# The differential-attention mixer of a two-block network: from projections first and attention second, to attention by pairs of heads beside the projections

## The reference, cut to what matters

```python
def mixer_ab(hx, hc, ...):      # 256 tokens, 256 context rows, D = 1024
    lam = exp(sum(lq1 * lk1)) - exp(sum(lq2 * lk2)) + lam_init
    q_x, k_x, v_x, gu_x, gv_x = split(hx @ w_in)     # 8 heads x 2 x 64; v: 8 x 128
    q_x, k_x = apply_rope(q_x), apply_rope(k_x)
    k_c, v_c = split(hc @ w_in[:, QK_W:2 * QK_W + V_W])
    k_all, v_all = concat(k_c, k_x), concat(v_c, v_x)        # 512 keys
    # per block of 128 queries and per head:
    p = softmax(q @ k.T * scale)             # two maps of 128 x 512
    a = p[:, :, 0] - lam * p[:, :, 1]
    o_x = a @ v
    a_x = o_x * rsqrt(mean(o_x * o_x) + eps) * norm_g * (1 - lam_init)   # per head
    u, v = gelu(gu_x), layer_norm(gelu(gv_x))
    g_x = u * (w_s @ v + b_s)
    return concat(a_x, g_x) @ w_out
```

## Time and profile before

| | |
|---|---|
| median of 3 runs | 2221.75 us (2221.7 to 2222.33) |
| profiled execution, its own time | 2223.49 us |
| its span | 2221.7 us |
| TensorE busy over the span | 1822.1 us (82%) |
| VectorE / ScalarE busy | 1471.4 us (66%) / 877.2 us (39%) |
| the mixer stage in it | 413.7 to 729.1 us |

### The profile page before, as it was taken

The page is one execution under the profiler, slowest core; times in us unless marked ns, Lnnn a source line. Parts: engine busy times, 40 slices in busy tenths (PEclk is TensorE's granted clock), DMA queues, the critical chain, the costliest instruction groups (busy, mean ns, idle before and its releaser), DMA issues.

```text
span 2221.7 us, 21883 instructions
## 1 busy us (share of the span) xinstructions
PE 1822.1 (82%) x7101; PEld 1095.4 (49%) x7101; DVE 1471.4 (66%) x3020; ACT 877.2 (39%) x2284; POOL 622.3 (28%) x567
## 2 busy tenths in 40 slices
PE   4887999899877688888877877996888788877886
PEld 3757998799756443434322332354444343322332
DVE  6767956855676657667667677525576777677755
ACT  3445433523343234334434444312343444444433
POOL 1160000000000333534353443203344344444441
PEclk7889989898988799999999999998999999999999
DMA  9653758546334499999999999944999999999996
GB/s 370 261 195 124 263 203 303 210 178 259 114 133 143 188 384 411 420 418 421 394 406 421 422 421 421 367 170 195 371 405 420 419 421 421 421 421 421 421 422 252
DMA packets 114690, 723.76 MB, mean 326 GB/s; under 512 B 11504, under 2 KB 13344, under 8 KB 34064
## 3 DMA queue, kind: packets, MB, share of 16 engines
q0 software_dynamic: 74864, 540.30, 58.8%
q1 hardware_dynamic: 39712, 182.07, 22.1%
HBM read 721.24 MB, written 1.08 MB: 325 GB/s over the span
## 4 chain that ended last, share of the span: by engine, by line
PE 40%; DMA 31%; DVE 19%; ACT 4%; issue 4%; POOL 1%; SPq 0%; DVEq 0%; ACTq 0%; POOLq 0%
DMA X<-in_k_uv,EI 16%; PE PS L1980 14%; DMA Z<-in_k_uv,EI 7%; DMA W<-in_peer_wq 5%; PE PS L1957 5%; PE PS L1672 4%; PE PS L1674 4%; PE PS L1673 4%; DVE junk L1659 4%; DVE ACC L1273 3%; DMA W<-in_ada_w 2%; DVE WL L1289 2%; PE PS L1760 2%; PE PS L2033 1%; PE PS L1995 1%
## 5 line engine op out<-in xcount | busy, mean ns | idle before, releaser
L1980 PE MATMUL PS<-X,dg 128*128 128x512 f32 x1372 | 666.4, 620 | 170.2 <-ACT dg L911 167.6
L1659 DVE CUSTOM_DVE_ANT_0 junk<-H,X 128x1024 f32<-128x1024 f32 x343 | 420.0, 1225 | 244.4 <-DMA X<-in_k_uv,EI 237.6
L902 POOL DMA_INDIRECT X<-in_k_uv,EI x343 | 376.7, 1098 | 620.8 <-PE PS L1980 360.3
L1980 PEld LDWEIGHTS PS<-X,dg 128*128 128x128 f32 x1372 | 247.1, 193 | 544.2 <-ACT dg L911 337.8
L911 ACT ACTIVATE CF<-DOT 128x1 f32<-128x1 f32 x512 | 102.2, 200 | 581.9 <-DVE DOT L1659 578.6
L1980 PE MATMUL PS<-Z,dg 128*128 128x512 f32 x504 | 248.8, 628 | 51.7 <-ACT dg L911 51.0
L911 ACT ACTIVATE dg<-CP,CG 128x128 f32<-128x128 f32 x512 | 205.5, 401 | 16.9
L1659 DVE CUSTOM_DVE_ANT_0 junk<-H,Z 128x1024 f32<-128x1024 f32 x126 | 154.3, 1225 | 86.9 <-DMA Z<-in_k_uv,EI 80.9
L1980 PEld LDWEIGHTS PS<-Z,dg 128*128 128x128 f32 x504 | 93.4, 197 | 190.4 <-ACT dg L911 111.1
L902 POOL DMA_INDIRECT Z<-in_k_uv,EI x126 | 138.5, 1099 | 140.9 <-PE PS L1980 120.0
L1672 PE MATMUL PS<-XH,WH 128*128 128x256 f32 x592 | 173.3, 293 | 4.2 <-DVE WL L1289 2.3
(11 more groups left out here) (294 smaller groups left out, 2636.7 us busy)
## 6 DMA issues: line engine op xcount, KB each, us to landing
W<-in_ada_w SPq DMA_DIRECT2D x51, 1024.0 KB, 6.2
Y<-in_ada_w SPq DMA_DIRECT2D x21, 1024.0 KB, 5.7
W<-in_peer_wq SPq DMA_DIRECT2D x16, 1024.0 KB
W<-in_k_ffi SPq DMA_DIRECT2D x13, 1024.0 KB, 6.0
Y<-in_k_ffi SPq DMA_DIRECT2D x9, 1024.0 KB, 4.9
Y<-in_k_win SPq DMA_DIRECT2D x9, 1024.0 KB, 8.3
W<-in_ffn_w_out SPq DMA_DIRECT2D x8, 1024.0 KB, 5.3
W<-in_k_win SPq DMA_DIRECT2D x7, 1024.0 KB, 6.9
```

Of the source, the lines that this page charges most:

```text
L902: e.indirect_dma_start(out=WS[k][:, :], out_offset=None, in_=I[f"k_uv{ly}"][:, :], in_offset=bass.IndirectOffsetOnAxis(ap=EI[t][:, j:j + 1 ...
L1659: e.tensor_tensor_reduce(junk, H[:, t, :], d[:, 0:D], 1.0, 0.0, ALU.mult, ALU.add, DOT[:, j:j + 1]).then_inc(v_dot, 1)
L1980: p = e.matmul(PS[:, 2 * t + q, :], dgb[n % 4][:, :], d[:, D + q * 512:D + (q + 1) * 512], start=(j == 0), stop=(j == 127))
```

## The change

The projection order becomes pair by pair: q, k and v of heads 0 and 1, then of heads 2 and 3, and so on, and the four gate tiles last. Attention units are ordered by head, the two query blocks of a head next to each other. The four units of a pair run among the twenty quarters of the next pair's projections, five quarters to a unit; the last pair's run among the sixteen quarters of the gate tiles, four to a unit. Projections alternate between PSUM banks 6 and 7; scores have banks 0 and 1 once, not twice; the turned map has bank 2, the output bank 3. ScalarE copies each unit's output to `OB` and squares it with a running sum; the head norm becomes two steps per pair of heads (`hs`, `hs2`), and `xt` 4 follows per head. `lam` moves ahead of `xt` 2. `ring3` moves ahead of the projections, so that the stage loads through W0 to W2 alone. `ldw` and `split` of part n+2 stand at the end of part n. Ada steps are dealt out one by one. `gate`, the layer norm of the gate (`gn` 2, 3) and rows 3 to 5 stand in the output parts, whose tile 3 comes last.

```diff
-WIN_ORDER = list(range(8)) + [14, 15, 12, 13] + list(range(8, 12))
+WIN_ORDER = [0, 4, 8, 1, 5, 9, 2, 6, 10, 3, 7, 11, 14, 15, 12, 13]
+AO_ORDER = [0, 1, 2, 4, 5, 3]
...
-    for c in range(8):
-        xt(2, c, bank(low))
+    P("ring3")
     P("ldctx")
     P("lam")
-    split(IN + 1)
...
     P("gn8")
     for c in range(8):
-        xt(4, c, bank(low))
+        xt(2, c, 4 + c % 4)
+    split(IN + 1)
+
+    def products():
+
+        group, rope, pend = 0, 0, None
+        for i in range(16):
+            n, tile = IN + i, WIN_ORDER[i]
+            for q in range(quarters(n)):
+                b = 6 + group % 2
+                P("gq", n, q, b)
+                if q in (2, 5) and pend is not None:
+                    P("rope2", *pend)
+                    pend = None
+                if q == 3:
+                    P("evac", n, b, rope)
...
+                if q == quarters(n) - 1:
+                    P("ldw", n + 2)
+                    split(n + 2)
+                yield
...
+    g = products()
+    for k in range(20):
+        if k < 8:
+            xt(3, k, k % 4)
+        if k % 5 == 4:
+            step(5)
+        next(g)
+    for n in range(16):
+        for k in range(5):
+            if k == 0:
+                P("ds", n)
+            elif k == 1 and n:
+                P("dt", n - 1)
+            elif k == 2 and n:
+                P("do", n - 1)
+                if n % 4 == 0:
+                    P("hs", n // 4 - 1)
+            elif k == 3:
+                P("dn", n)
+                if n >= 4 and n % 4 == 1:
+                    P("hs2", n // 4 - 1)
+            elif k == 4 and n >= 4 and n % 4 in (2, 3):
+                h = 2 * (n // 4 - 1) + n % 4 - 2
+                P("xp", 4, h, 4)
+                P("xt", 4, h, 4)
+                P("xl", 4, h)
+            if k == 1 or k == 4 and n < 12 and n % 2:
+                step(5)
+            if n >= 14 and k == 3:
+                P("gn", n - 14)
+            if n in (6, 7, 8) and k == 2:
+                row(2, n - 6, 5)
+            if k or n < 12:
+                next(g)
+    for _ in g:
+        pass
+    P("gn", 2)
+    P("gn", 3)
...
+    g = part(0)
+    P("dt", 15)
+    next(g)
+    P("gate", 0, 1)
+    next(g)
+    P("do", 15)
+    P("hs", 3)
...
+    for w in (3, 4, 5):
+        P("rowv", w)
+        step(2)
+        g = part(w - 1)
+        next(g)
+        row(w, 1, 0)
+        next(g)
+        row(w, 2, 1)
```

More of the change, by code:

```diff
@@ new lines, in make_plan, with step @@
+    steps = iter(range(43, 72))
+    mods = {47: 6, 55: 7, 63: 8, 71: 9}
+    due = []
+    def step(b):
+        while due:
+            mod(due.pop(), b)
+        m = next(steps, None)
+        if m is not None:
+            ada(m)
+            if m in mods:
+                due.append(mods[m])
+    g = products()
[32 more added lines that the diff above has]
+                next(g)
@@ new lines, in make_plan, with part @@
+    for _ in g:
+        pass
+    P("gn", 2)
+    P("gn", 3)
+    def part(i):
+        n = AO + i
+        for q in range(4):
+            P("gq", n, q)
+            yield
+        if i < 4:
+            P("ldw", n + 2)
+            split(n + 2)
+    g = part(0)
[6 more added lines that the diff above has]
+    next(g)
+    P("gate", 1, 0)
+    next(g)
+    next(g, None)
+    P("hs2", 3)
+    g = part(1)
+    next(g)
+    P("gate", 2, 1)
+    next(g)
@@ L260, in make_plan @@
+    P("gate", 3, 0)
+    next(g)
+    P("xp", 4, 6, 2)
+    P("xt", 4, 6, 2)
+    P("xl", 4, 6)
+    next(g)
+    P("xp", 4, 7, 3)
+    P("xt", 4, 7, 3)
+    P("xl", 4, 7)
+    next(g, None)
+    for w in (3, 4, 5):
+        P("rowv", w)
+        step(2)
+        g = part(w - 1)
+        next(g)
+        row(w, 1, 0)
+        next(g)
+        row(w, 2, 1)
+        for _ in g:
+            pass
+    step(2)
     P("fold", 0)
     P("sc", 0)
[L262 to L272, removed]
+    for _ in part(5):
+        pass
@@ L672, in build @@
         units = [(s2, i, t) for s2 in range(2) for i in range(4) for t in range(2)]
-        order = [(t, hd) for t in range(2) for hd in range(8)]
+        order = [(t, hd) for hd in range(8) for t in range(2)]
         d_cp, d_x, d_sm, d_sm2, d_tab, d_sk, d_td, d_be = (sem("d_" + n) for n in (
@@ L1089, in _ @@
                     w.wait_ge(p_part, AO)
-                    act(GSH[:, g, :], XT[:, (32 + g) % 3, :], ACT.Copy).then_inc(a_xth, 1)
+                    act(GSH[:, g, :], XT[:, (nth.use["gate", g] - 1) % 3, :], ACT.Copy).then_inc(a_xth, 1)
                 elif kind == "ds":
@@ L1305, in _ @@
                     src, dh, dl, scale, bias = XTS[i]
-                    u = xuse(i, c)
+                    u = nth.use["xt", i, c] - 1
                     if c % 2 == 0:
@@ L1716, in out_part @@
                     k, t = t, k
-                kk = 2 * i + k
-                xh, xl = x(kk, t)
+                xh, xl = x(2 * r + k, t)
+                first, last = 2 * i + k == 0, 2 * i + k == nk - 1
                 split_half(n, k)
@@ L1733, in xin @@
             def xin(i, t):
-                return both(XH, XL)(i, t) if i < 8 else both(GSH, GSL)(i - 8, t)
+                if i < 8:
+                    turned(4, i)
+                    return chunk(XTS[4][1], i, t), chunk(XTS[4][2], i, t)
+                w.wait_ge(a_xth, nth.use["gate", i - 8])
+                w.wait_ge(v_xtl, nth.use["gate", i - 8])
+                return chunk(GSH, i - 8, t), chunk(GSL, i - 8, t)
             for kind, *a in plan:
```

275 lines of the change are left out of this document (159 added, 116 removed), and 2 rows, old and new, of tables (d_gath, p_x).

## The result

| | kernel before | changed kernel |
|---|---|---|
| median of 7 runs | 2221.75 us (2218.71 to 2225.87) | 2232.41 us (2229.31 to 2235.80) |
| ratio to before | | 1.0044, 95% interval 1.0031 to 1.0058 |
| profiled execution, its own time | 2223.49 us | 2235.80 us |
| from the end of the last `XS` to the residual norm | 413.7 to 729.1, 315.4 us | 415.4 to 742.4, 327.0 us |

The changed kernel is slower by some 10 us, and the interval excludes no change. The prediction was 2235. In the profiled execution the stage began 1.7 us later than before, ahead of anything that the change touches, and is 11.6 us longer; the rest of the program takes what it took. So the stage is compared by its length. This execution is the slowest of the changed kernel's seven, 3.4 us above their median, so every length that is taken off its 327.0 comes out some 3 us too large.

The account below looks back on a forecast made before the run. TensorE was taken to bound the projections, a chain across engines the attention. 464.3 + 157.2 + 58.4 + 62.4 put the residual norm at 742.3 against 729.06, +13, so 2235 us; range 2207 to 2254.

Parts of the forecast that it names:

- The start, +11: Before unit 0: late turned input and late context chunks start unit 0 at 464, where densely it would be 453.
- The `lam` half: At the start: `XT` waits for the lambda row until about 421.7, 7.2 us later; part 0 ends 5.5 us late.
- The other half: At the start: a late weight load and split delay context chunks to 447.6; quarter 5 of the second part waits about 5.
- Units 0 to 11, +22: Middle units: waits of 0.5 us ahead of `do`, 3.2 where a split precedes the maximum; 157.2 us, densely 135 to 137.
- Units 12 to 15, +25: Last four units: TensorE stands 4.7 us at `do` in each, behind a split; 58.4 us, densely 33.
- "below 0.85": Sign to look for in the last four units: TensorE's granted clock under 0.85.
- The tail, 62.4: Output parts: 49.3 us of work, 6.3 waiting for the gate's norm and 6.8 for broadcast rows.
- T: Rival, (d) in the prediction: 8 extra ScalarE table loads end on TensorE's path at 1.28 us each, +10, 2245; chance 0.11.
- The sum of stalls, 71 against 58 of dense gain: Whole stage: stalls of 11 + 22 + 25 + 13 = 71 us, where the gain without any would be about 58.
- rival (a): Whole stage: overlap holds and the kernel is faster; with half the stalls 2200, with none 2164; chance 0.22.
- The ring, priced at nothing: Three load slots for five cost nothing in the forecast; rival (c) had late loads add 15 to 30, 2258, chance 0.09.
- Tables: Units 12 to 15: the table load after the split ends at 4.0, before the maximum at 5.6, so costs nothing.

Follow-up runs that it names:

- the splits' move: Changed kernel with splits whose part ends in a unit's last quarter put behind the next unit's `do` step: 2219.41 us, ratio 0.9995 to the kernel before.
- the three groups: Changed kernel with `lam` behind `xt` 2, late splits behind `do`, and gate norm and rows ahead of splits in the tail: 2206.51 us, ratio 0.9930.
- the fourth move: The `do` step one quarter later in TensorE's queue, put on top of the three groups: 2187.67 us against 2206.51.
- the four: Changed kernel with the three groups and the fourth move together: 2187.67 us, ratio 0.9846 to the kernel before.

## Why the prediction was right

The outcome, 2235 forecast and 2232.4 measured, and its mechanism held: queue order, not work, is what the interleaved units lose by. That the sum came within 3 us is in part luck: against lengths of 50.6, 157.2, 58.4 and 62.4 the trace has 47.1, 155.6, 59.3 and 65.0, so that a miss of 3.5 at the start and one of 2.6 in the tail cancel, and within units 0 to 11 two larger ones do. By its steps:

- **The start, +11.** The `lam` half held in kind: `XT` waits for the lambda row. That it came at 421.89 where 421.7 was said is luck, since the stage itself began 1.7 later; counted from there `XT` came 5.7 us later than before and not 7.2, because the row landed in 4.8 us and not 6.3. Putting `lam` back gives 4.0 (ratios) to 6.6 (stage), of which 2.4 had arrived when unit 0 started. The other half was wrong: quarter 5 was to wait 5 us for context chunks, and TensorE waited 0.95 there. The last chunks were ready at 446.5, 31.1 us into the stage where 33.9 were worked out, and TensorE came to them some 1 us later than I had it. The start was 47.1 us by the trace, 50.6 in the sum.
- **Units 0 to 11, +22.** 155.6 measured, 157.2 in the sum, but by two errors against each other. The waits for `AT` are 10.5 us, where 3.2 five times and 0.5 eleven times were counted, 21.5. Only one unit per pair has its split ahead of the maximum with nothing between: a part that ends with the fourth quarter leaves one more quarter before the next scores, and I counted it like one that ends with the unit. And TensorE's work was 145 us and not 135 to 137: the clock was 0.94, and 145 times 0.94 is 136.
- **Units 12 to 15, +25.** 59.3 measured, 58.4 in the sum; waits of 3.30, 4.26, 4.26 and 5.19 for 4.7 four times; clock 0.84, as "below 0.85" had it. This is the largest term, and the splits' move confirms its cause: the waits of these four units fell from 17.0 to 8.2.
- **The tail, 62.4.** 65.0 measured. The gate's wait 6.91 for 6.3, the rows' 8.1 for 6.8; moving both gives 10 to 11. Of the gate's 6.91, 0.9 was a table load (see T above).
- **The sum of stalls, 71 against 58 of dense gain.** By the experiments the three groups are worth 25 to 30 us, and the fourth move 18.8 beyond them. The trace bears the 71 out: the stage is 69.4 us longer than the 257.6 that the sum has without stalls, 49.8 of it without work and the rest work at the lower clock. The dense bound that rival (a) used (2164 with no stall) is not reached, but at 2187.67 the greater part of the way is shown: rival (a)'s mechanism is there, it only was not in this order.
- **The ring, priced at nothing.** Right for the changed plan by its waits, for a reason that I had not named: the same ring costs 47 us in the plan of before.
- **Tables.** Priced at nothing in the last four units. I placed only the load behind the split; in unit 15 another stands ahead of the evacuation and cost 0.9 us there, and 0.9 at the gate. The stage has 14 loads where it had 7; the eighth of the 91 lies outside it.

## What to carry to other kernels

Work that is dealt out between the steps of a chain must go behind the step on which the pacing engine waits next, on every engine that the chain crosses: here two subtractions of 1.2 us each, one place too early in VectorE's queue in six of sixteen units, cost 11 to 13 us. When a chain cannot be made shorter, let the engine that waits ask later; one quarter of dense work put ahead of `do` was worth 16 us alone, more than any single repair, and 19 on top of all three. Count the quarters between a part's end and the next step before charging a stall, and cost a smaller ring for the order in which its loads stand, not by bandwidth.

## What the runs showed of the hardware

TensorE's clock fell in places where TensorE was not idle at all. The third `mod`, 32 matmuls of one column each, ran from 612.39 to 616.0 in the changed kernel, full projection work stood on either side, and the clock fell behind it and came back some 4 us later. The first two rows below are the same behind the start of the first `mod` (473.96) and behind the second (540.09). The granted clock is the column ahead of the last two:

```profile
476.50:483.50 7.00, 7.00 (x29) 5.97 (x30) 2.09 (x4) 0.38 (x1) 0.00 (x0) 0.52 0.56 207
544.00:548.50 4.50, 4.50 (x28) 4.50 (x27) 2.67 (x3) 3.12 (x7) 0.00 (x0) 0.62 0.52 164
612.00:616.00 4.00, 4.00 (x38) 4.00 (x38) 0.42 (x1) 0.98 (x2) 0.00 (x0) 1.00 0.05 20
616.00:618.00 2.00, 2.00 (x13) 1.87 (x12) 1.37 (x2) 0.00 (x0) 0.00 (x0) 0.67 0.00 0
618.00:620.00 2.00, 2.00 (x5) 0.51 (x4) 0.22 (x1) 1.79 (x3) 0.00 (x0) 0.50 0.77 201
620.00:622.20 2.20, 2.20 (x18) 1.89 (x16) 2.20 (x3) 0.69 (x1) 0.00 (x0) 0.98 0.71 298
625.50:629.00 3.50, 3.50 (x22) 3.50 (x23) 1.83 (x8) 2.25 (x6) 0.00 (x0) 0.70 0.83 290
640.00:645.00 5.00, 5.00 (x31) 5.00 (x31) 2.09 (x8) 1.82 (x4) 0.00 (x0) 0.66 0.84 261
734.00:742.00 8.00, 8.00 (x53) 7.16 (x53) 3.77 (x5) 0.00 (x0) 0.00 (x0) 1.00 0.86 325
```

Not every `mod` is followed by a fall. The last row holds the fourth (734.51), with the clock at 1.00, and the first `mod` of the kernel with `lam` back ran at 1.00 too (its row stands there). The two rows ahead of the last are behind the waits of 3.30 and 4.26 us in units 12 and 13: there too the fall comes after the work has begun again. Between the third `mod` and the scores of unit 12, twice as long as others, stands no wait at all, so no stall just ahead accounts for these; that the `mod` does is what the order in time suggests, and no run moved or removed one. I had charged the clock to the stalls of 4 us alone.

Removing waits gave back somewhat more than their length. From the changed kernel to the four, TensorE's time without work fell by 33.3 us and its busy time by 11.4, the same work at 0.93 of the clock and not 0.89. How much of that the two kinds of fall had, and how much is only the difference between executions, was not separated.
